# Rounding, zeros, gated norms and a first model's last norm in another order, in a two-model kernel on one Trainium2 core

## The reference: what is computed

```python
# first model: depth 2
h = h + moba_nsa_mixer(rmsnorm(h), ...)     # attention of two kinds, relative-position bias
h = h + sqrelu_mlp(rmsnorm(h), w1, w2)      # 1024 -> 4096 -> 1024
h = h + fox_mixer(rmsnorm(h), ...)          # attention with forget gates
h = h + sqrelu_mlp(rmsnorm(h), w1, w2)
x = rmsnorm(h, final_norm)                  # the first model's last norm
# second model: depth 1, modulated by c
n = rmsnorm(x, g_ffn1) * (1 + sc1) + sh1;  h = x + 0.5 * gt1 * swiglu(n)   # 1024 -> 2816 -> 1024
n = rmsnorm(h, g_mix)  * (1 + sc2) + sh2;  h = h + gt2 * hybrid_mixer(n)
n = rmsnorm(h, g_ffn2) * (1 + sc3) + sh3;  h = h + 0.5 * gt3 * swiglu(n)
return rmsnorm(h, g_final)
```

## Time and profile before

| | us |
|---|---|
| median of three runs | 1099.05 |
| the profiled execution, whole | 1098.95 |
| its span, first to last instruction | 1097.2 |
| PE busy in the span | 1076.2 |
| DVE busy | 778.6 |
| ACT busy | 660.4 |
| POOL busy | 115.5 |

### The profile page before, as it was taken

How to read it: one execution, slowest core, us unless ns; L and a number is a source line. 1 busy time by engine, 2 the same in 40 slices (tenths; PEclk the granted TensorE clock), 3 DMA queues, 4 the chain that set the end, 5 groups by cost and what they waited for, 6 DMA issues and landing times.

```text
span 1097.2 us, 15918 instructions
## 1 busy us (share of the span) xinstructions
PE 1076.2 (98%) x6098; PEld 918.3 (84%) x6098; DVE 778.6 (71%) x1261; ACT 660.4 (60%) x1067; POOL 115.5 (11%) x209
## 2 busy tenths in 40 slices
PE   8999999999999999999999999999999999999997
PEld 7898788888888998888888788888878978888885
DVE  6767667777786776687676777887875766565566
ACT  6667676565666776766565754354475766444443
POOL 2033101010100531020000000110000200000000
PEclk9999999999999999999999999999999999999999
DMA  9842348878864643687778467768545344555551
GB/s 341 298 158 79 115 156 326 304 289 306 300 217 173 212 140 113 217 306 279 255 277 312 154 227 289 294 244 312 188 165 183 131 154 173 192 191 183 185 183 64
DMA packets 40619, 238.30 MB, mean 217 GB/s; under 512 B 4661, under 2 KB 5845, under 8 KB 17632
## 3 DMA queue, kind: packets, MB, share of 16 engines
q1 hardware_dynamic: 26784, 188.81, 48.3%
q0 software_dynamic: 13040, 47.85, 11.7%
q10 hardware_dynamic: 720, 0.62, 0.2%
HBM read 236.15 MB, written 1.11 MB: 216 GB/s over the span
## 4 chain that ended last, share of the span: by engine, by line
PE 81%; DVE 9%; ACT 5%; issue 3%; DMA 1%; POOL 0%; DVEq 0%; ACTq 0%
PE bank L1570 20%; PE bank L1539 13%; PE bank L1541 13%; PE bank L1540 13%; PE bank L1571 10%; PE bank L1694 2%; DVE w_lo L1070 2%; PE bank L1758 1%; ACT w_hi L699 1%; PE bank L1740 1%; DVE ada_raw L1300 1%; PE bank L1732 1%; PE bank L1588 1%; PE bank L1589 1%; PE bank L1592 1%
## 5 line engine op out<-in xcount | busy, mean ns | idle before, releaser
L1570 PE MATMUL bank<-a_two,w_hi 128*128 128x512 f32 x1088 | 386.9, 399 | 0.8 <-DVE w_lo L1070 0.8
L1070 DVE TENSOR_TENSOR w_lo<-raw,w_hi 128x2048 fp32r<-128x2048 f32 x122 | 278.4, 2303 | 107.2 <-ACT w_hi L699 107.1
L1571 PE MATMUL bank<-a_two,w_lo 128*128 128x256 f32 x1088 | 305.5, 281 | 0.0
L699 ACT ACTIVATE w_hi<-raw 128x2048 fp32r<-128x2048 f32 x122 | 232.2, 1910 | 63.5 <-DMA raw<-in_stream 63.4
L1570 PEld LDWEIGHTS bank<-a_two,w_hi 128*128 128x128 f32 x1088 | 204.5, 188 | 51.0 <-issue 1.4
L1571 PEld LDWEIGHTS bank<-a_two,w_lo 128*128 128x128 f32 x1088 | 205.7, 189 | 1.7
L1539 PE MATMUL bank<-w_lo,hid_hi 128*128 128x512 f32 x432 | 169.6, 393 | 0.3 <-DVE w_lo L1070 0.2
L1540 PE MATMUL bank<-w_hi,hid_lo 128*128 128x512 f32 x432 | 168.7, 390 | 0.0
L1541 PE MATMUL bank<-w_hi,hid_hi 128*128 128x512 f32 x432 | 168.6, 390 | 0.0
L871 ACT ACTIVATE cross<-bank 128x256 f32<-128x256 f32 x136 | 51.5, 381 | 186.2 <-PE bank L1571 186.1
L1059 DVE TENSOR_TENSOR w_lo<-raw,w_hi 128x1024 fp32r<-128x1024 f32 x104 | 125.5, 1229 | 22.3 <-ACT w_hi L688 22.2
(11 more groups left out here) (231 smaller groups left out, 1478.4 us busy)
## 6 DMA issues: line engine op xcount, KB each, us to landing
raw<-in_stream SPq DMA_DIRECT2D x173, 1024.0 KB, 5.0
ada_raw<-in_ada POOLq DMA_DIRECT2D x72, 512.0 KB, 5.3
cmpw<-in_stream SPq DMA_DIRECT2D x4, 1024.0 KB, 8.1
rel_band<-rel_scratch POOLq DMA_DIRECT2D x2, 1024.0 KB, 7.2
cum_row<-cum_scratch POOLq DMA_DIRECT2D x4, 512.0 KB, 4.8
gate_row<-gate_scratch POOLq DMA_DIRECT2D x3, 512.0 KB, 5.8
h<-in_x SPq DMA_DIRECT2D x2, 512.0 KB, 4.3
raw<-in_stream SPq DMA_DIRECT2D x2, 512.0 KB, 7.0
```

Source lines behind the costliest of these rows:

```text
L699: nc.scalar.activation(w_hi[:, u % RING, :], raw[:, u % RING, :], ACT.Copy).then_inc(hi_ready, 2)
L1070: nc.vector.tensor_tensor(w_lo[:, u % RING, :], raw[:, u % RING, :], w_hi[:, u % RING, :].bitcast(F32), ALU.subtract).then_inc(lo_ready, 2)
L1570: nc.tensor.matmul(ps[bank][:, 0:2 * T], wh[:, k, cols_], a_two[:, :, k, :], start=k == 0, stop=False)
L1571: ins = nc.tensor.matmul(ps[bank][:, T:2 * T], wl[:, k, cols_], a_hi[:, k, :], start=False, stop=k == KT - 1)
```

## The change

Four edits, none of which adds or drops arithmetic.

1. POOL waits for `lo_ready` 6 (three units split) before it writes the zeros.
2. At the start ACT takes chunk 3 of both token halves and the two halves of unit 3 ahead of the copy of the bias rows, instead of behind it.
3. In the passages "gmix" and "gf2", `gated_turn` stands for `norm_turn`. On DVE the shift of chunk 3 goes behind the addition of the last quarter of `h`, chunk 1 ahead of it, and the first mean ahead of chunk 2; chunk 3 goes behind the root. On ACT the squares and the root of t = 1 go ahead of chunk 3, and the rounding of a half unit behind both.
4. The first model's last norm takes one half row at each of the steps j = 2, 3, 4, 5.

```diff
@@ -601,6 +601,7 @@
             pool.dma_start(rpick[:, :], rel_pick).then_inc(pick_landed, 16)
             pool.dma_start(bfor[:, :], b_forget).then_inc(bfor_landed, 16)
             pool.wait_ge(pool_step, 1)
+            pool.wait_ge(lo_ready, 6)
             zeros(slice(0, 6), 0)
             pool.wait_ge(rel_rows_sb, 1)
             pool.dma_start(rel_dram[:, 0:REL], rrow[:, :]).then_inc(rel_stored, 16)
@@ -764,6 +765,21 @@
                 inv = fin[:, t, 12:13] if name == "gf1" else stat[:, 7, t:t + 1]
                 for c0, c1 in ((0, 256), (256, 512), (512, 1024)):
                     nc.scalar.activation(tok[:, t, c0:c1], h[:, t, c0:c1], ACT.Copy, scale=inv).then_inc(rows_scaled_act, 1)
+
+            def gated_turn(name, gain, shift):
+
+                squares(name, 0)
+                round_half()
+                scale(name, 0)
+                turned(name, 0, gain, shift, (0, 1))
+                square_half(name, 1, 0)
+                turned(name, 0, gain, shift, (2,))
+                square_half(name, 1, 1)
+                root(name, 1)
+                turned(name, 0, gain, shift, (3,))
+                round_half()
+                scale(name, 1)
+                turned(name, 1, gain, shift)
 
             def norm_turn(name, gain, shift=None):
 
@@ -935,10 +951,12 @@
                 turned("mix0", t, gain0, chunks=(2,))
             round_half()
             round_half()
+            for t in range(TT):
+                turned("mix0", t, gain0, chunks=(3,))
+            round_half()
+            round_half()
             act.wait_ge(rel_rows, 1)
             nc.scalar.activation(rrow[:, :], ps[4][0:16, 0:REL], ACT.Copy).then_inc(rel_rows_sb, 1)
-            for t in range(TT):
-                turned("mix0", t, gain0, chunks=(3,))
             advance(FIRST["v_even"] + 4)
 
             def even_extras(tick):
@@ -998,7 +1016,7 @@
-            norm_turn("gmix", gainc[:, KT:2 * KT], modc[:, 3 * KT:4 * KT])
+            gated_turn("gmix", gainc[:, KT:2 * KT], modc[:, 3 * KT:4 * KT])
@@ -1025,7 +1043,7 @@
-            norm_turn("gf2", gainc[:, 2 * KT:3 * KT], modc[:, 6 * KT:7 * KT])
+            gated_turn("gf2", gainc[:, 2 * KT:3 * KT], modc[:, 6 * KT:7 * KT])
@@ -1086,12 +1104,16 @@
                     chain(nc.vector.tensor_tensor(tok[:, t, half], ps[bank][:, :], gate[:, half], ALU.mult))
                     nc.vector.tensor_tensor(to, to, tok[:, t, half], ALU.add).then_inc(h_ready, 1)
 
-            def inverse_root(name, t):
-
+            def first_mean(name, t):
+
+                dve.wait_ge(sumsq, squares_before(name, t) + 1)
+                nc.vector.tensor_scalar(stat[:, 2, t:t + 1], stat[:, 0, t:t + 1], EPS[name], None, ALU.add).then_inc(mean_ready, 1)
+
+            def inverse_root(name, t, first_taken=False):
                 n = NORM[name]
                 first, v, y, b = (stat[:, i, t:t + 1] for i in (2, 4, 5, 6))
-                dve.wait_ge(sumsq, squares_before(name, t) + 1)
-                nc.vector.tensor_scalar(first, stat[:, 0, t:t + 1], EPS[name], None, ALU.add).then_inc(mean_ready, 1)
+                if not first_taken:
+                    first_mean(name, t)
                 dve.wait_ge(mean_ready, n + t + 1)
                 dve.wait_ge(sumsq, squares_before(name, t) + 2)
                 chain(nc.vector.tensor_scalar(v, stat[:, 1, t:t + 1], first, -0.5, ALU.add, ALU.mult))
@@ -1150,20 +1172,23 @@
                 polish(t, 9, 11, 14, 15)
                 chain(nc.vector.scalar_tensor_tensor(out=f[:, 13:14], in0=f[:, 15:16], scalar=1.5, in1=f[:, 14:15], op0=ALU.add, op1=ALU.mult))
 
-            def turned(name, t, gain, shift=None, chunks=(0, 1, 2, 3)):
+            def shift_chunk(name, t, c, gain, shift):
 
                 m = TURN[name] + 4 * t
+                dve.wait_ge(bank_turned, m + c + 1)
+                if t == 1:
+                    dve.wait_ge(act_split, m - 4 + c + 1)
+                for kt in (2 * c, 2 * c + 1):
+                    ins = nc.vector.tensor_scalar(shifted[:, c, kt % 2, :], ps[TURN_BANKS[name][t][c]][:, (kt % 2) * P:(kt % 2 + 1) * P],
+                                                  gain[:, kt:kt + 1], shift[:, kt:kt + 1], ALU.mult, ALU.add)
+                ins.then_inc(rows_shifted, 1)
+
+            def turned(name, t, gain, shift=None, chunks=(0, 1, 2, 3), shifts=True):
+
                 ts = slice(t * P, (t + 1) * P)
                 for c in chunks:
-                    if shift is not None and c < 2:
-                        odd = 2 * c + 1
-                        dve.wait_ge(bank_turned, m + odd + 1)
-                        if t == 1:
-                            dve.wait_ge(act_split, m - 4 + odd + 1)
-                        for kt in (2 * odd, 2 * odd + 1):
-                            ins = nc.vector.tensor_scalar(shifted[:, odd, kt % 2, :], ps[TURN_BANKS[name][t][odd]][:, (kt % 2) * P:(kt % 2 + 1) * P],
-                                                          gain[:, kt:kt + 1], shift[:, kt:kt + 1], ALU.mult, ALU.add)
-                        ins.then_inc(rows_shifted, 1)
+                    if shift is not None and c < 2 and shifts:
+                        shift_chunk(name, t, 2 * c + 1, gain, shift)
                     dve.wait_ge(act_high, split_no(name, t, c))
                     bank, c0 = turned_at(name, t, c)
                     if shift is not None:
@@ -1177,6 +1202,24 @@
                                 out=a_lo[:, kt, ts], in0=ps[bank][:, c0 + (kt % 2) * P:c0 + (kt % 2 + 1) * P],
                                 scalar=gain[:, kt:kt + 1], in1=a_hi[:, kt, ts].bitcast(F32), op0=ALU.mult, op1=ALU.subtract)
                     ins.then_inc(act_split, 1)
+
+            def gated_turn(name, sums, gain, shift, gate):
+
+                for k in range(2):
+                    add(name, sums, gate, 0, k)
+                inverse_root(name, 0)
+                rest_half()
+                add(name, sums, gate, 1, 0)
+                shift_chunk(name, 0, 1, gain, shift)
+                turned(name, 0, gain, shift, (0, 1), False)
+                add(name, sums, gate, 1, 1)
+                shift_chunk(name, 0, 3, gain, shift)
+                first_mean(name, 1)
+                turned(name, 0, gain, shift, (2,))
+                inverse_root(name, 1, True)
+                turned(name, 0, gain, shift, (3,))
+                rest_half()
+                turned(name, 1, gain, shift)
 
             def norm_turn(name, sums, gain, shift=None, gate=None):
 
@@ -1272,12 +1315,11 @@
                 nc.vector.tensor_tensor(hid_lo[:, slot, :], hid_f[:, :], hid_hi[:, slot, :].bitcast(F32),
                                         ALU.subtract).then_inc(hid_ready, 1)
 
-            def last_norm(t):
-
-                for k in range(2):
-                    half = slice(512 * k, 512 * k + 512)
-                    nc.vector.scalar_tensor_tensor(out=h[:, t, half], in0=h[:, t, half], scalar=fin[:, t, 13:14], in1=row[:, half],
-                                                   op0=ALU.mult, op1=ALU.mult).then_inc(h_final, 1)
+            def last_norm(t, k):
+
+                half = slice(512 * k, 512 * k + 512)
+                nc.vector.scalar_tensor_tensor(out=h[:, t, half], in0=h[:, t, half], scalar=fin[:, t, 13:14], in1=row[:, half],
+                                               op0=ALU.mult, op1=ALU.mult).then_inc(h_final, 1)
 
             def gains(names):
 
@@ -1357,9 +1399,10 @@
                             modulation_column(p)
                         if (name, j) == ("glu0", FF2 - 2):
                             gains(("gf2",))
-                        if name == "glu0" and j in (2, 4):
-                            first_norm_root(j // 2 - 1)
-                            last_norm(j // 2 - 1)
+                        if name == "glu0" and 2 <= j < 6:
+                            if j % 2 == 0:
+                                first_norm_root(j // 2 - 1)
+                            last_norm(j // 2 - 1, j % 2)
 
             nc.vector.memset(probT[:, 0, 0:P], 0.0).then_inc(zeros_set, 1)
             nc.vector.memset(kc[:, :, :, 15:16].bitcast(F32), 0.0)
@@ -1488,7 +1531,7 @@
-            norm_turn("gmix", "glu0", gainc[:, KT:2 * KT], modc[:, 3 * KT:4 * KT], gate_row)
+            gated_turn("gmix", "glu0", gainc[:, KT:2 * KT], modc[:, 3 * KT:4 * KT], gate_row)
@@ -1508,7 +1551,7 @@
-            norm_turn("gf2", "out_dil", gainc[:, 2 * KT:3 * KT], modc[:, 6 * KT:7 * KT], gate_row)
+            gated_turn("gf2", "out_dil", gainc[:, 2 * KT:3 * KT], modc[:, 6 * KT:7 * KT], gate_row)
```

## The result

The changed kernel takes 1091.78 us (median of 6 runs, 1091.4 to 1092.68) against 1098.70 (6 runs, 1097.13 to 1100.7) for the kernel before: ratio 0.9938, 95% interval 0.9925 to 0.9951. It is faster, by 6.9 us or 0.6%, and the interval leaves no doubt of it. The forecast was 1094.5; the time lies 0.2 us under the low end of the range, 1092.0.

A forecast was written before the change was run, and what follows sets the result against it. PE was taken as the bound, busy 1076.2 of 1097.2 us, so only its idle time could be won. The terms 0.65 + 1.60 + 1.56 + 0.65 = 4.46 us, taken from 1098.95, gave 1094.5; range 1092.0 to 1097.0.

The forecast's parts named there:

- Zeros later: At the start, DVE's slow line 1109 drops from 1.155 to 0.47 us without the memset beside it: 0.65 us.
- about 10.0: Sign at the start: PE's transposes of t = 1 would begin at about 10.0 us, instead of 10.70.
- Unit 3: At the start, PE's wait for unit 3's `w_lo` at 29.26 goes wholly: 1.60 us.
- Gated passages: In gf2 and gmix, ACT's scaling starts earlier, with the half unit the next limit: 0.79 and 0.77 us.
- The last norm: In glu0, the wait at j = 2 ends and about 0.4 stays at j = 4: 0.65 us.
- The clock, not in the sum: PE's two lower-clock stretches, at 12.8 to 16.1 and 907.05 to 910.00, cost about 1.5 us each; left uncounted.
- The clock comes back: Rival, start and gf2: one slow stretch regained gives 1093.0 us, both 1091.5; chance 0.22.
- the other half: Rival that the clock falls elsewhere, gf1's wait being untouched: one more slow stretch 1096.0 us, two 1097.5; chance 0.13.
- The start was not given back: Rival: a later stage paced by loads loses the start's 2.25 us, giving 1096.7; chance 0.10.
- The passages won what was said: Rival for gmix and gf2: ACT and DVE in lockstep over chunk 3 and mean win nothing, 1096.1 us; chance 0.10.
- The slower case: Rival: PE's clock stays low behind every short wait, five more slow stretches, 1102.0 us; chance 0.03.

The follow-up runs named there:

- gated_only: The kernel before with only the new order in gmix and gf2: mean 1095.71 us (9 runs), ratio 0.9972.
- fill_gf2: The kernel before with four unused matmuls of 512 columns added in PE's wait in gf2: mean 1097.88 us (10 runs).
- all_but_gated: The kernel before with zeros later, unit 3 ahead and the last norm in four, without the gated passages' order: mean 1094.95 us, ratio 0.9956.
- after_again: The changed kernel unaltered, run again: mean 1093.26 us (6 runs), ratio 0.9952 against the kernel before.
- after_no_zeros: The changed kernel without POOL's added wait for `lo_ready` 6: mean 1093.69 us (5 runs), ratio 0.9956 against the kernel before.
- the start's filler: Unused matmuls of 128 columns between the transposes of t = 0 and t = 1; ten of them alone in the kernel before: mean 1099.74 us (11 runs).
- fill_three: The kernel before with four unused matmuls of 512 columns in each of gf1, gmix and gf2: mean 1097.03 us (12 runs).
- the better version: The changed kernel, ACT's half unit before chunk 1 in gmix and gf2, DVE's chunk 3 subtraction behind gf1's inverse root: mean 1090.95 us (10 runs).
- fill_four: The kernel before with unused matmuls in four PE waits, at the start and in gf1, gmix and gf2: mean 1097.81 us (11 runs).

## Why the prediction was right and wrong

The sum of the work held. The changed kernel has 12 runs in all, mean 1092.60; 8 are high, mean 1092.00. Before has 1096.53 in its high runs: 4.53 us, where the sum said 4.46. (These high runs lie within 1.9 and 1.4 us, so a difference of their means is good to about 0.5; that it comes to 0.07 is luck.) By its terms:

- **Zeros later, 0.65.** Line 1131 takes about 483 ns four times. PE's transposes start at 10.26, 0.44 earlier, behind a scaling that began 0.22 later: 0.66 at an equal start. The forecast's "about 10.0" is missed by that lateness. That they wait 1.61 instead of 1.87 measures nothing, since `gated_only` has 1.60 with its memset where it was. The memsets in their new place cost nothing. The Trainium skill (SBUF — State Buffer, "Who interferes with whom") says that a DVE instruction with two SBUF inputs contends with a GpSimd instruction that reads SBUF, and not with one that only writes it; the trace agrees, with 2.29 us for `w_lo` beside the memsets and 2.29 alone.
- **Unit 3, 1.60.** PE's unit 2 starts 1.78 us earlier (23.22 to 21.44) and unit 3 3.38 earlier: 1.60, to the hundredth. The first matmul came at 25.88, not 27.0, since the start's clock (1.35) was not in that number, nor the 0.22 by which the start came later.
- **Gated passages, 0.79 and 0.77.** The waits fell by 0.74 (gf2) and 0.72 (gmix). The half unit was the next limit, as worked out, and chunk 2 held nobody up.
- **The last norm, 0.65.** No wait at j = 2, 0.30 at j = 4; 0.66 in the table above.
- **Not foreseen, some 0.4.** Before waited 0.19 for `w_lo` at 611.13, the changed kernel's trace not at all, which is worth 0.35 by the prediction's own count. In the other traces this wait is anything from none to 1.61, for kernels that differ in nothing near it. So I put it down to the execution, not to the change; what sets it I didn't test.

**The step that failed is "The clock, not in the sum".** The prediction found both low stretches, priced one at about 1.5 us, saw that the idle time in front of both gets shorter, and then took both at nothing in the sum, with 0.22 for the case in which they come back. They came back in all six of the first runs, for 1.35 us at the start and 1.4 behind gf2: the rival "The clock comes back", both stretches, had 1091.5, the profiled execution took 1091.4. That this is so near is in part luck, as the six runs held no low stretch anywhere. The reason against it was that 626 to 630 stayed fast behind a wait of the same length. That was one execution. Over the traces gf1 does get the low stretch (`fill_gf2`, `fill_start`, `all_but_gated`, `after_again`, `after_no_zeros`), so the row was no counterexample but one draw. The start's wait, too, was read as one number, 1.87, where other traces with the memset in its old place have 1.06 to 2.27. Right was the other half, that a low stretch stays possible behind the waits that are left: 4 of the 12 runs of the changed kernel are below 0.998, and the one of them that has a trace has it in gf1. Priced as what it is, an expectation, the clock costs before 1098.79 - 1096.53 = 2.26 us on average, and the changed kernel 1092.60 - 1092.00 = 0.60; 1.7 us belonged into the sum. With it the forecast is 1092.8, and the mean of 12 runs 1092.6. And a range that leaves out a case of 0.22 in part has to end beyond that case: 1091, not 1092.0.

The Trainium skill (TensorE: Matmul & The Clock Gate, "What's actually happening") says of a kernel's first matmuls that how many of them run at the lower clock differs between runs of the same kernel. The runs agree, and show it in the middle of a kernel too: before has clocks from 0.993 to 0.999, and the stretch was seen behind each of four waits. I used it only to call the question open. It should have led to the mean over executions.

**The other rivals.** The start was not given back: 3.38 us at unit 3 were 3.96 at gf1. The passages won what was said. The slower case had nothing for it: no run of the changed kernel is over 1095.39.

**Left open.** Why the start's filler costs 1.1 us in high runs; what makes the wait at 611 differ; what decides which of several long waits is hit in an execution; and whether PE's wait at unit 3 (1.44), behind which no trace has a low stretch, ever has one.

## What to carry to other kernels

Read PE's clock as a risk that each wait carries: list the waits of about 1.5 us and more in front of dense matmuls, the ones that stayed fast included, and put into the sum the share of runs that suffer times the price. Bring each of them down, even where it can't be removed, since the last one left still hits some runs. Judge an edit of a few us by runs of equal mean clock as well as by the median; here that turned 6.9 us into 4.5 of work and the rest of clock and luck. And look at a wait in more than one trace before you say that an edit changed it.

## What the runs showed of the hardware

- Work of no use can pay: `fill_three` has twelve matmuls more than before, all of them for nothing, and is 1.6 us faster in the mean of its job (1097.03 against 1098.61; ratio 0.9987, 0.9978 to 0.9995).
- The 16 low stretches of 19 traces stood only behind waits of PE of 1.45 to 2.27 us (start, gf1, gmix, gf2), never behind one of 1.2 or less, the end of the program left aside. Not every long wait has one: gf1's of 1.53 or 1.54 had it in 5 of 12 traces.
- A spread of 4 to 6 us between executions of one kernel can be mostly clock: before's 108 runs lie within 5.8 us and its 12 high runs within 1.9, and the ten runs of the better version, with its waits short, within 1.0. The clock is not all of it: the 11 runs of `fill_four`, all high, lie within 2.5 us.
- PE's wait for `w_lo` at about 611 us was anything from none to 1.61 us in 19 traces, with the same code around it.
